# Probability blocks split in two and held stationary in the sparse-attention stage of a hybrid decoder block

## What is computed

```
def _dsa_attention(q, k, v, q_idx, k_idx, w_idx, slopes, topk):
    ...                                             # k, v: (B, S, 64), shared by the 8 heads
        _, sel = lax.top_k(score, topk)             # 256 keys for each query
        logits = jnp.einsum('bthd,btkd->bhtk', qb, k_sel).astype(jnp.float32) * scale
        logits = logits - slopes[None, :, None, None] * dist[:, None]
        logits = jnp.where(valid[:, None], logits, -jnp.inf)
        p = jax.nn.softmax(logits, axis=-1)
        return jnp.einsum('bhtk,btkd->bthd', p.astype(v.dtype), v_sel)
```

## The kernel before

| step | PE logits of row i | DVE minimum of i | ACT exponential of i | units |
|---|---|---|---|---|
| 5 | 0 | 2 | 3 | u0 u1 |
| 6 | 7 | 1 | 2 | u2 u3 |
| 7 | 6 | 0 | 1 | u4 u5 |
| 0 | 5 | 7 | 0 | u6 u7 |
| 1 | 4 | 6 | 7 | l0 |
| 2 | 3 | 5 | 6 | l1 |
| 3 | 2 | 4 | 5 | l2 |
| 4 | 1 | 3 | 4 | l3 |

## Time and profile before

### The profile page before, as it was taken

How to read it: one execution, slowest core, us unless ns; L and a number is a source line. 1 busy time by engine, 2 the same in 40 slices (tenths; PEclk the granted TensorE clock), 3 DMA queues, 4 the chain that set the end, 5 groups by cost and what they waited for, 6 DMA issues and landing times.

```text
span 1446.6 us, 18529 instructions
## 1 busy us (share of the span) xinstructions
PE 1341.9 (93%) x6181; PEld 1071.7 (74%) x6181; DVE 1021.0 (71%) x1464; ACT 683.7 (47%) x1153; POOL 722.7 (50%) x624
## 2 busy tenths in 40 slices
PE   2899999998899999997998899999999999999997
PEld 2668888776566666665876778888888888887886
DVE  4778699988867655553675986666666666368787
ACT  5456677736676655554115633222323234354332
POOL 3134454556677866550002165555555556578552
PEclk9899899998999999998999999999999999999999
DMA  9521244456533344315453244444444445989432
GB/s 326 177 63 30 88 131 130 145 175 189 131 91 100 106 114 118 86 37 197 157 170 117 87 143 163 167 168 167 168 153 145 149 144 197 356 295 327 156 110 117
DMA packets 123562, 220.20 MB, mean 152 GB/s; under 512 B 9386, under 2 KB 52500, under 8 KB 123220
## 3 DMA queue, kind: packets, MB, share of 16 engines
q1 hardware_dynamic: 123476, 219.12, 45.9%
HBM read 160.90 MB, written 57.93 MB: 151 GB/s over the span
## 4 chain that ended last, share of the span: by engine, by line
PE 42%; DVE 7%; issue 2%; DMA 1%; ACT 1%; POOL 0%; DVEq 0%; POOLq 0%; SPq 0%; ACTq 0%
PE ps_out L2288 26%; PE ps_out L2314 12%; PE ps_out L1641 1%; PE ps_out L1625 1%; DVE mod_acc_final L1708 1%; DMA scr_mod_final<-mod_acc_final 1%; DVE y_full L1729 1%; ACT square_junk L2206 0%; DVE x L2550 0%; DVE y_gated L1741 0%; DVE down_part L2548 0%; DVE wgu_lo L2395 0%; PE ps_out L1649 0%; DVE wo_lo_sb L1692 0%; DVE h_sum_t L2362 0%
## 5 line engine op out<-in xcount | busy, mean ns | idle before, releaser
L1985 POOL TENSOR_TENSOR wgu_lo<-wgu_raw,wgu_hi 128x512 fp32r<-128x512 f32 x66 | 97.2, 1481 | 127.6 <-ACT wgu_hi L1977 127.6
L2222 POOL TENSOR_TENSOR dn_lo<-dn_raw,dn_hi 128x512 fp32r<-128x512 f32 x77 | 126.6, 1662 | 67.4 <-ACT dn_hi L2128 67.4
L1977 ACT ACTIVATE wgu_hi<-wgu_sum 128x512 fp32r<-128x512 f32 x88 | 55.2, 632 | 200.0 <-DVE wgu_sum L2378 80.0
L2288 PE MATMUL ps_out<-h_b_t_hi,wgu_hi 128*128 128x512 f32 x352 | 138.3, 393 | 6.7 <-DVE h_b_t_lo L2366 2.6
L2288 PE MATMUL ps_out<-h_b_t_lo,wgu_hi 128*128 128x512 f32 x352 | 137.6, 391 | 0.0
L2288 PE MATMUL ps_out<-h_b_t_hi,wgu_lo 128*128 128x512 f32 x352 | 137.6, 391 | 0.0
L483 POOL TENSOR_TENSOR win_lo<-win_raw,win_hi 128x256 fp32r<-128x256 f32 (+1 forms) x84 | 66.4, 821 | 139.0 <-ACT win_hi L473 115.5
L2128 ACT ACTIVATE dn_hi<-dn_raw 128x1024 fp32r<-128x1024 f32 x77 | 81.2, 1062 | 114.4 <-PE ps_out L2314 55.7
L2314 PE MATMUL ps_out<-dn_hi 128*128 128x512 f32 x308 | 120.4, 391 | 0.0
L2314 PE MATMUL ps_out<-dn_hi,dn_lo 128*128 128x512 f32 x308 | 119.9, 389 | 0.0
L2314 PE MATMUL ps_out<-dn_lo,dn_hi 128*128 128x512 f32 x308 | 119.9, 389 | 0.0
(11 more groups left out here) (346 smaller groups left out, 3650.9 us busy)
## 6 DMA issues: line engine op xcount, KB each, us to landing
scr_act_sums<-act_sums SPq DMA_DIRECT2D x11, 1792.0 KB, 6.9
dn_raw<-scr_act_sums SPq DMA_DIRECT2D x77, 256.0 KB, 5.3
wmod_c<-in_w_mod_dram SPq DMA_DIRECT2D x48, 256.0 KB, 2.9
wgu_raw<-in_w_gate_dram SPq DMA_DIRECT2D x11, 1024.0 KB, 5.5
wgu_raw<-in_w_up_dram SPq DMA_DIRECT2D x11, 1024.0 KB, 5.4
wd_sums<-in_w_down_dram SPq DMA_DIRECT2D x11, 1024.0 KB, 4.8
scr_wd_sums<-wd_sums SPq DMA_DIRECT2D x11, 1024.0 KB, 4.1
dn_raw<-scr_wd_sums SPq DMA_DIRECT2D x44, 256.0 KB, 7.0
```

Of the source, the lines that this page charges most:

```text
L1985: pool.tensor_tensor(sl[slot(m, x)][:], src, sh[slot(m, x)][:].bitcast(F32), ALU.subtract).then_inc(wlp, 1)
L2222: pool.tensor_tensor(bl[q % NSLOT][:, 1], braw[entry(q)][:, 1], bh[q % NSLOT][:, 1].bitcast(F32), ALU.subtract).then_inc(dlw, 1)
L2288: last = pe.matmul(bank(m, b), a[s][:, t], h[x][t // 2][:, t % 2], start=(fresh and t == 0 and a is sh and h is hh), stop=(t == 3 and a is ...
```

## The change

The probabilities and v are each split into a part rounded to fp32r and the rest, and the product is made of three fp32r products in place of one in full float32. The roles are turned: a 128x128 block of the transposed unit is stationary, high part and then low part, and v moves: 128 columns (high and low parts side by side) against the high part, 64 columns against the low one. The output then stands by tokens (queries on partitions, 4 blocks of 2 x 64 columns). DVE adds the two column halves, in two instructions, and divides there with a third. For a pair's two heads together PE transposes the result once (kind "o", two steps after the group's end, when the pair's second head ends), and ACT copies it to `of`. All sparse units are now copied by ACT (high part) and then subtracted by DVE (low part), and the place is free after the subtraction. At steps 0 and 4 DVE makes its minimum after the subtractions and no longer before. `spread` with its matmuls and copies is gone. In the phase before, POOL makes v's low part in place of a second copy of v, after ACT has made the high part.

```diff
-            pool.wait_ge(kvt, NT)
-            pool.tensor_copy(g.vd[:, :, HD:P], rl[:, 0].rearrange("p (b d) -> p b d", b=NT)[:, :, HD:P]).then_inc(vdc, 1)
+            pool.wait_ge(vdc, 1)
+            pool.tensor_tensor(g.vd[:, :, HD:P], rl[:, 0].rearrange("p (b d) -> p b d", b=NT)[:, :, HD:P],
+                               g.vd[:, :, 0:HD].bitcast(F32), ALU.subtract).then_inc(vdc, 1)
...
-        return v, [("s", gr) for gr in range(SBG, 2 * SBG) if end.get(gr, -99) == r]
+        return v, [("o", gr) for gr in range(SBG, 2 * SBG) if gr % 4 >= 2 and end.get(gr, -99) + 2 == r]
...
scalar:
             for n in of_step[r]:
-                if not by_act(n):
+                if not by_act(n) and not sparse(n):
                     continue
...
-                act.activation(aT[:, n % NA, s], place(("u", n))[:, s], ACT.Copy).then_inc(cpa, 1)
-            for gr in spread(r):
-                act.wait_ge(sd, d + 1)
-                act.activation(spr[lanes, upper(gr)], place(("s", gr))[lanes], ACT.Copy).then_inc(sc, 1)
+                act.activation((aTh if sparse(n) else aT)[:, n % NA, s], place(("u", n))[:, s], ACT.Copy).then_inc(cpa, 1)
+            for gr in turned(r):
+                act.wait_ge(ott, pairs_done(gr) + 1)
+                act.wait_ge(olr, out_index(gr) - 1)
...
+                act.activation(of[:, upper(gr)], place(("o", gr)), ACT.Copy).then_inc(ofc, 1)
...
vector:
-            elif r < NR:
...
+            elif r < NR and r % 4:
+                minima(r)
             for n in of_step[r]:
-                if by_act(n):
+                if by_act(n) and not sparse(n):
                     continue
...
-                dve.tensor_copy(aT[:, n % NA, s], place(("u", n))[:, s]).then_inc(cpd, 1)
+                if sparse(n):
+                    dve.wait_ge(cpa, act_copies(n))
+                    dve.tensor_tensor(aTl[:, n % NA, s], place(("u", n))[:, s], aTh[:, n % NA, s].bitcast(F32),
+                                      ALU.subtract).then_inc(cpd, 1)
...
+            if SBR <= r < NR and r % 4 == 0:
+                minima(r)
...
-                    dve.wait_ge(sc, gr - SBG + 1)
-                    dve.tensor_tensor(of[lanes, G], o[lanes], spr[lanes, G], ALU.mult).then_inc(od, 1)
+                    dve.tensor_copy(mine, parts[:, :, 0]).then_inc(oad, 1)
+                    dve.wait_ge(oad, d + 1)
+                    dve.tensor_tensor(mine, parts[:, :, 1], mine, ALU.add).then_inc(od, 1)
+                    dve.wait_ge(od, gr + 1)
+                    dve.wait_ge(rc, d + 1)
+                    dve.tensor_tensor(mine, mine, rs[:, 4 * d:4 * d + 4].unsqueeze(2).to_broadcast([P, 4, HD]),
+                                      ALU.mult).then_inc(otn, 1)
...
tensor:
-                v = vs[:, gr // 4 % 2, b] if gr < SBG else g.vd[:, b]
-                pe.matmul(o[:, s], v, aT[:, n % NA, s], start=(b == 0), stop=(b == 4 * upper(gr) + 3),
-                          skip_group_check=True).then_inc(vd, 1)
-            for gr in spread(r):
...
+                else:
+                    for q in range(left(n) // P, 4):
+                        x = slice(P * q, P * q + P)
+                        pe.matmul(o[:, x], aTh[:, n % NA, x], g.vd[:, b], start=(b == 0 and q == 0), stop=True,
+                                  skip_group_check=True)
+                        last = pe.matmul(o[:, P * q:P * q + HD], aTl[:, n % NA, x], g.vd[:, b, 0:HD], start=False,
+                                         stop=True, skip_group_check=True)
+                    last.then_inc(vd, 1)
+            for gr in turned(r):
+                await_freed(follows["o", gr])
+                pe.wait_ge(otn, gr - SBG + 1)
+                for q in range(4):
+                    last = pe.transpose(place(("o", gr))[:, P * q:P * q + P],
+                                        ot[:, upper(gr), q].rearrange("p h d -> p (h d)"), g.ident[:])
+                last.then_inc(ott, 1)
```

More of the change, by code:

```diff
@@ L1032, in attention @@
     prod = at("mod_prod_c", [P, HALF], 36)
-    spr = at("rsum_spread", [P, 2, HALF], 51)
+    aTh = at("aT_hi", [P, NA, HALF], 24, F32R)
+    aTl = at("aT_lo", [P, NA, HALF], 49, F32R)
+    ot = at("o_tokens", [P, 2, 4, 2, HD], 57)
     with ExitStack() as ctx:
@@ L1066, in attention @@
     rc = k.sem("d_rsum_ready")
-    sd = k.sem("rsum_spread_done")
-    sc = k.sem("rsum_spread_copied")
+    oad = k.sem("d_o_parts_added")
+    otn = k.sem("d_o_normalised")
+    ott = k.sem("d_o_transposed")
+    ofc = k.sem("d_o_copied")
     oll = k.sem("oT_lo_last_ready")
@@ L1080, in by_act, with sparse, act_copies, dve_copies @@
         return b % 2 == (0 if upper(gr) or gr < SBG else 1)
+    def sparse(n):
+        return units[n][0] >= SBG
+    def act_copies(n):
+        return sum(sparse(m) or by_act(m) for m in range(n + 1))
+    def dve_copies(n):
+        return sum(sparse(m) or not by_act(m) for m in range(n + 1))
     def copied(n):
-        return cpa if by_act(n) else cpd, sum(by_act(m) == by_act(n) for m in range(n + 1))
+        return (cpa, act_copies(n)) if by_act(n) and not sparse(n) else (cpd, dve_copies(n))
+    def pairs_done(gr):
+        return 2 * ((gr - SBG) // 4) + gr % 2
     def left(n):
@@ L1091, in ended, with turned @@
         return [gr for gr in end if end[gr] + steps == r]
-    def spread(r):
-        return [gr for gr in end if gr >= SBG and end[gr] == r]
+    def turned(r):
+        return [gr for gr in end if gr >= SBG and gr % 4 >= 2 and end[gr] + 2 == r]
     def paired(r, steps):
@@ L1239, in scalar @@
                 n = out_index(gr)
-                act.wait_ge(od, gr + 1)
+                if stage:
+                    act.wait_ge(ofc, pairs_done(gr) + 1)
+                else:
+                    act.wait_ge(od, gr + 1)
                 act.activation(hi[:, pair, x], of[:, G], ACT.Copy).then_inc(ohr, 1)
@@ L1298, in vector, with minima @@
         dve.wait_ge(cset, 1 + NPB)
+        def minima(r):
+            y, gr = r - SBR, r // 4
+            h, i = rows[y]
+            w = P * (i + 1)
+            if y == 0:
+                dve.wait_ge(mul, SBR)
+                dve.wait_ge(p1.sl, p1.SL_ALL)
+            dve.wait_ge(zr, y + 1)
+            dve.wait_ge(td, done_by[gr - 2])
+            dve.tensor_tensor_reduce(a[gr % 2][:, i % 4, 0:w], z[:, r % NZ, 0:w], g.score[:, soff(i):soff(i + 1)],
+                                     g.nslope[:, h:h + 1], 3e38, ALU.add, ALU.min,
+                                     nm[:, y:y + 1]).then_inc(tt, 1)
         for r in range(STEPS):
@@ L1366, in await_freed @@
                 pe.wait_ge(v_rdy, n + 1)
-            elif kind == "s":
-                pe.wait_ge(sc, n - SBG + 1)
+            elif kind == "o":
+                pe.wait_ge(ofc, pairs_done(n) + 1)
             else:
@@ L1451, in tensor @@
                         pe.wait_ge(od, gr)
-                v = vs[:, gr // 4 % 2, b] if gr < SBG else g.vd[:, b]
-                pe.matmul(o[:, s], v, aT[:, n % NA, s], start=(b == 0), stop=(b == 4 * upper(gr) + 3),
-                          skip_group_check=True).then_inc(vd, 1)
-            for gr in spread(r):
[L1456 to L1463, removed]
+                if gr < SBG:
+                    pe.matmul(o[:, s], vs[:, gr // 4 % 2, b], aT[:, n % NA, s], start=(b == 0),
+                              stop=(b == 4 * upper(gr) + 3), skip_group_check=True).then_inc(vd, 1)
+                else:
+                    for q in range(left(n) // P, 4):
[12 more added lines that the diff above has]
+                last.then_inc(ott, 1)
     p = Programs(sync, scalar, gpsimd, tensor, vector)
```

33 lines of the change are left out of this document (14 added, 19 removed).

## The result

The changed kernel takes 1484.38 us (median of 4, 1478.41 to 1493.59) beside 1449.2 for the one before: ratio 1.0243, 95% interval 1.0211 to 1.0275. The forecast had the sign and a sum of +14.7 us; the time lies above its range. The profiled execution took 1478.41 us, its span is 1476.7. It is the fastest of the four; the others, at 1482.48, 1486.28 and 1493.59, have a granted clock of 0.947, 0.947 and 0.937 over the whole execution beside its 0.952. So what follows accounts for 30.1 us, and what the median has above that is in no trace.

What follows compares the result with a forecast made beforehand. PE set the pace before; afterwards waits in the ACT and DVE chain would. First head 0.7, first heads with turns 5.75, second heads 5.4, last 0.5, end 2.3: +14.7 us on 1448.33 gives 1463.0; range 1443 to 1472.

Steps and rivals of the forecast that it cites:

- The chain: Sparse heads: each unit goes PE, ACT, DVE, PE in series, so a head takes 21.0 us, 0.7 more.
- a turn at step 6: First head of a pair: ACT waits for PE's transposing of the finished output, delaying later copies; +1.25 us.
- the turn at step 2: Second head of a pair: ACT's late turned-output copy delays exponentials and DVE's minimum of i = 3; +0.95 us.
- its signs: What the profile would show, among it 21 to 22.5 us between 640-key minima, against 20.3 before.
- PE's short matmuls: Products in the sparse heads: matmuls with their own weight loads start 0.11 us apart, 7.9 us a head.
- The subtraction and the group's end: DVE in the sparse heads: 0.681 us per subtraction; three steps of 0.45 each, 1.35, at an ended group.
- The end: Last head +0.5 us from the same waits; last product to last addition 6.2 us in place of 3.9, +2.3.
- The cover in the phase before: Before the stage: POOL's subtraction comes 1.3 us later but is hidden, costing nothing; 1.3 if the cover failed.
- The turns: Transposing finished pairs' outputs: ACT's queue waits for PE, +1.25 or +0.95 us each, three of each kind.
- the sentence on the clock: Sparse stage: clock stays full, with PE 17 of 22 us busy and no stop above 1.3; a fall given 0.02.
- the faster rival of the forecast: ACT's and DVE's chain keeps ahead of PE, which stays the bound: heads of 18.9 us, 1439 in all; chance 0.17.

Runs made afterwards that it cites:

- e1: Changed kernel with the low part of each block moving v's 128 columns in place of 64; 1475.53 us, ratio 1.0202.
- e9: Changed kernel with 128 columns for the low part, turned-output copy a step later, two orders changed, useless matmuls ahead of two waits and in the last head; 1460.82 us.
- e3: Changed kernel plus 11 useless PE matmuls of 512 columns a head, just ahead of three of PE's waits; 1474.4 us, ratio 1.0194.
- e8: Kernel before with the split alone: v's parts stationary, probabilities' parts moving, copies by ACT then subtractions by DVE; spread and output as before; 1458.25 us.
- e2: Changed kernel without subtractions: ACT and DVE share units, one copy each, both products take the high part, low part left out; 1443.76 us, ratio 0.997.
- e7: Changed kernel with 128 columns for the low part and four useless matmuls of 512 columns in each step of the last head; 1477.67 us.

## Why the prediction was wrong, step by step

**The chain was right in place, and in size for a pair of heads.** At full clock the heads cost +12.3 (e1) for +11.9: the first +1.5 for +0.7, since before it took 18.98 and not the 20.34 that the forecast gave it, and the other six +10.8 for +11.15. Times of one head with a turn at step 6, in us from the end of its 640-key minimum (550.07 in e1):

| | forecast | e1 |
|---|---|---|
| ACT starts the exponential of i = 3 | 2.2 | 2.65 |
| ACT starts the copy of the turned output | 8.5 | 8.84 |
| PE starts u6 | 12.65 | 12.76 |
| PE starts u7 | 14.0 | 14.20 |
| PE starts l0's product | 19.8 | 19.99 |
| next end of that minimum | 22.3 | 22.43 |

This column is the forecast's first head with the 1.25 of its own turn. The 0.95 that the forecast put on the turn at step 2 of the head before falls behind that head's 640-key minimum, so it would arrive in this one. The forecast's terms thus give 21.2 and 23.2 in turn (among its signs it wrote 21 to 22.5), where e1 has 21.3 to 21.8 and 22.4 to 22.8: right in the sum of two, too far apart.

**PE's short matmuls, 0.11 each:** right (0.22 a pair). **The subtraction and the group's end:** right within 0.01 and 0.03 us. **The end:** last head and end +4.5 for +2.8 in the changed kernel; e9, with a little filler, two orders changed and the clock at 1.00 up to 675 us, has +2.8. **The cover in the phase before:** held. **The turns:** the heads with them are longer by about what was said, but cutting ACT's waits for the turn from 14.1 us to 3.2 gave back only 0.0 to 0.4 of each, so the mechanism given, ACT's queue, was wrong for most of it, and what takes its place is open.

**The step that failed is the sentence on the clock.** It read "PE at 16.08 of 20 us kept it in full, and it fell from 2.4 GHz towards 1.2 (0.74 on average) only with PE still for 6.5 us", and gave the fall 0.02. The row was right and did not carry the inference. Those 16 us were for the most part matmuls of 256 to 512 columns, and among them the clock stayed at 1.00 over a stop of PE twice as long as any in the changed heads:

```profile
360.00:363.50 3.50, 1.21 (x12) 0.97 (x10) 3.50 (x5) 1.45 (x4) 3.42 (x3) 1.00 0.49 136
...
363.50 0.66 PE L1437 MATMUL ps_z<-ident,a_rows 128*128 128x128 f32 x4 [2.29 <-DVE aT L1331]
```

After the change PE was still for 1.1 us at most at a time in the heads, as the forecast had said (no stop above 1.3), and the clock fell all the same, which cost 18 us in the heads. e3 shows it is a cause of time and no bystander, since work that is thrown away made the heads 12 us shorter in all. What it takes was not settled. Waits of PE alone do not do it (e8 has eight of 1.0 us for the same cause at 1.00, and the row above one of 2.29), nor do the short matmuls alone (e2, at 1.00 in five of seven heads). Where both come together it falls at some of the stops: in the changed kernel, in both profiled executions, and in e2 at one stop of two. With 128 columns for 64 it does so sometimes (e7) and sometimes not (e1).

**The sum, put right:** +12.3 for the chain and the turns, +18.1 for the clock in the heads, +4.5 in the last head and the end, 34.9 in the stage; 4.8 less elsewhere, which no run explains and which lies within what the rest of the span varies (1277.7 to 1285.8).

**What the change was worth without its series and the instructions that go with it:** e2's 17.6 us against e1 in the seven heads. That is the faster rival of the forecast, and its condition (the chain ahead of PE) was named rightly: 135.7 us for seven heads is 19.4 each for 18.9. But no kernel here has that and the low part too.

## What to carry to other kernels

When a copy out of PSUM becomes two instructions on two engines in series, follow one period through every queue before counting PE's work: with PE's new work alone (e2) a head was 0.75 us shorter than before, with the subtractions behind the copies (e1) it was 1.8 longer. When long matmuls are cut into short ones with a weight load each, do not take the clock for granted because PE's busy share stays high; price the stage at the lower level too, and keep some weight on it. And fill a wait that PE has to make with work that is due anyway: two changed orders gave back 0.7 to 0.9 us a head here.

## What the hardware showed that I had not expected

The granted clock fell to 0.50 for 10 us and more while PE's records show it busy without a pause (540 to 550 us). The same head code ran at 1.00 in e1 and, in five of seven heads, at 0.80 to 0.93 in e7, so the clock depends on more than the code of the head. DVE's multiplication with both operands in SBUF (128x256) took 0.42 us mostly but 0.87 at 530.48, 1.26 at 574.61 and 0.80 at 629.82, mean 0.550. These three ran for 0.5 us and more beside an instruction of POOL on SBUF, and none that ran without POOL took above 0.43; but e1 has one of 0.42 (at 569.95) with a POOL addition beside it all the time, so this is no rule. The two that read PSUM stayed at 0.40 and 0.43. Short matmuls with a weight load each started 0.11 apart whether 64 or 128 columns moved in fp32r, or a single one.
